# Two of eight tiles of a projection are moved ahead of the transposes that they stood behind

## The reference

```python
q, k, v = qkv_heads(h, w_qkv)                       # h @ w_qkv, 16 heads of 64
def one_chunk(c):                                   # 64 queries see a band of 9 chunks of keys
    s = jnp.einsum('bqhd,bkhd->bhqk', q_c, k_c).astype(jnp.float32) * scale + bias
    s = jnp.where(valid, s, NEG)
    p = jax.nn.softmax(s, axis=-1).astype(v.dtype)
    return jnp.einsum('bhqk,bkhd->bqhd', p, v_c)
```

## Time and profile before

| | |
|---|---|
| median of 3 runs | 2464.14 us (2463.99 to 2464.99) |
| profiled execution, its own time | 2464.97 us |
| its span, first to last instruction | 2463.2 us |
| granted clock of TensorE | 0.998 of full speed |
| busy: VectorE, ScalarE, POOL | 1546.7, 906.8, 231.2 us |

### The profile page before, as it was taken

One profiled execution on the slowest core, in us unless ns is written; L12 is line 12 of the kernel. 1 busy time (PEld: TensorE's weight loads), 2 busy tenths in 40 slices (PEclk: granted clock), 3 DMA queues, 4 the chain that ended last, 5 costly groups with the idle time before them and its releaser, 6 DMA issues.

```text
span 2463.2 us, 42975 instructions
## 1 busy us (share of the span) xinstructions
PE 2438.4 (99%) x16495; PEld 2392.2 (97%) x16495; DVE 1546.7 (63%) x2853; ACT 906.8 (37%) x1709; POOL 231.2 (9%) x535
## 2 busy tenths in 40 slices
PE   8999999999999999999999999999999999999998
PEld 8999999999999999999999999999999999999998
DVE  5666666677866666666666724427666666666666
ACT  6455545455433222222333641325222223322223
POOL 1011111103000000000000321221000000000000
PEclk9999999999999999999999999999999999999999
DMA  6122222444111111111111211112111111111112
GB/s 168 54 61 61 61 61 61 133 143 135 52 52 51 51 34 34 34 51 51 51 51 35 71 35 35 37 51 69 46 41 34 51 51 51 51 51 43 34 42 81
DMA packets 136522, 145.37 MB, mean 59 GB/s; under 512 B 4444, under 2 KB 125956, under 8 KB 136420
## 3 DMA queue, kind: packets, MB, share of 16 engines
q1 hardware_dynamic: 120420, 118.69, 15.2%
q0 software_dynamic: 14384, 23.03, 3.6%
q10 hardware_dynamic: 1616, 2.25, 0.3%
HBM read 125.97 MB, written 17.97 MB: 58 GB/s over the span
## 4 chain that ended last, share of the span: by engine, by line
PE 95%; DVE 2%; ACT 2%; issue 0%; DMA 0%; DVEq 0%; ACTq 0%
PE psum L170 29%; PE psum L169 29%; PE psum L171 29%; PE psum L1055 2%; PE psum L1075 2%; PE psum L1020 2%; PE psum L1984 1%; DVE w_lo L777 1%; DMA raw<-in_a_w_qkv 0%; PE psum L1968 0%; ACT w_hi L773 0%; PE psum L913 0%; ACT pB L1199 0%; ACT pA L1199 0%; DVE raw L2353 0%
## 5 line engine op out<-in xcount | busy, mean ns | idle before, releaser
L169 PE MATMUL psum<-gx_hi,w_hi 128*128 128x352 f32 x3456 | 1123.8, 325 | 1.3 <-DVE gx_lo L231 0.8
L170 PE MATMUL psum<-gx_lo,w_hi 128*128 128x352 f32 x3456 | 1116.3, 323 | 0.0
L171 PE MATMUL psum<-gx_hi,w_lo 128*128 128x352 f32 x3456 | 1115.2, 323 | 0.0
L169 PEld LDWEIGHTS psum<-gx_hi,w_hi 128*128 128x128 f32 x3456 | 649.8, 188 | 3.6 <-issue 1.0
L170 PEld LDWEIGHTS psum<-gx_lo,w_hi 128*128 128x128 f32 x3456 | 650.0, 188 | 0.6
L171 PEld LDWEIGHTS psum<-gx_hi,w_lo 128*128 128x128 f32 x3456 | 649.8, 188 | 0.0
L1743 DVE TENSOR_TENSOR x<-x,psum 128x352 f32<-128x352 f32 x528 | 258.4, 518 | 119.1 <-PE psum L171 118.9
L1614 ACT ACTIVATE conv_t<-a_gate,cur 128x352 f32<-128x352 f32 x132 | 89.9, 681 | 539.5 <-DVE a_gate L1694 532.3
L170 PE MATMUL psum<-h_loB,w_hi 128*128 128x352 f32 x528 | 171.1, 324 | 0.0
L171 PE MATMUL psum<-h_hiB,w_lo 128*128 128x352 f32 x528 | 171.0, 324 | 0.0
L170 PE MATMUL psum<-h_loA,w_hi 128*128 128x352 f32 x528 | 170.9, 324 | 0.0
(11 more groups left out here) (194 smaller groups left out, 2941.3 us busy)
## 6 DMA issues: line engine op xcount, KB each, us to landing
raw<-in_f_w_up SPq DMA_DIRECT2D x44, 1024.0 KB, 5.1
raw<-in_f_w_down SPq DMA_DIRECT2D x22, 1024.0 KB, 4.9
raw<-in_a_w_o SPq DMA_DIRECT2D x25, 512.0 KB, 4.0
raw<-in_a_w_qkv SPq DMA_DIRECT2D x22, 512.0 KB, 3.8
raw<-in_b_w_in SPq DMA_DIRECT2D x8, 1024.0 KB, 5.6
raw<-in_b_w_out SPq DMA_DIRECT2D x4, 1024.0 KB, 5.2
gx_hi<-o_scratch POOLq DMA_DIRECT2D x3, 1232.0 KB, 7.3
gx_lo<-o_scratch POOLq DMA_DIRECT2D x3, 1232.0 KB, 9.7
```

The costliest lines, as they stand in the source:

```text
L169: pe.matmul(out, w[0], rhs[0], start=first, stop=False)
L170: pe.matmul(out, w[0], rhs[1], start=False, stop=False)
L171: return pe.matmul(out, w[1], rhs[0], start=False, stop=last)
```

## The change

In steps that have no value products (step 1 and the even steps up to 62) the first two tiles of the projection are issued ahead of the first two groups of turns, the other six at the old place. `projection` takes the tiles as an argument; qkv_done is raised by the last tile. Both calls carry the waits for lin_out and at_lo. The work of the other engines is the same in the same order.

```diff
+    AHEAD = 2
+
...
-        def projection(t, s):
+        def projection(t, s, tiles):
 
             u, c = divmod(s, NCH)
             n = QKV0 + 3 * t + u
             pe.wait_ge(lin_out, STEPS * (t + 1) + s)
             pe.wait_ge(at_lo, n + 1)
-            linear(pe, psum[:, 7, :CH[c][1]], w_hi[n % 2], w_lo[n % 2], c).then_inc(qkv_done, 1)
+            mm = linear(pe, psum[:, 7, :CH[c][1]], w_hi[n % 2], w_lo[n % 2], c, None, tiles, KT - 1 in tiles)
+            if KT - 1 in tiles:
+                mm.then_inc(qkv_done, 1)
...
+            ahead = AHEAD if 1 <= g <= STEPS * LAST and not weighed(g) else 0
+            if ahead:
+                projection(*step_of(g - 1), range(ahead))
             if 1 <= g <= ALL:
                 turn(g - 1, range(min(2, len(key_groups((g - 1) % STEPS)))))
...
             elif g <= STEPS * LAST:
-                projection(*step_of(g - 1))
+                projection(*step_of(g - 1), range(ahead, KT))
```

## The result

The changed kernel took 2472.17 us (median of 8 runs, 2470.42 to 2472.97) against 2464.22 before (8 runs): 8.0 us more, a ratio of 1.0031 with a 95% interval of 1.0022 to 1.0040. Slower, by more than the forecast 6.7 us and inside the range. The profiled execution took 2472.04, 7.07 over that of before. Two of the twelve executions of experiment 2 took 6168 us, which no trace here explains, and are left out of its median.

What follows compares the result with a forecast made beforehand. TensorE, busy 99% of the span, was taken to bound the kernel. 3.4 + 1.3 + 1.7 + 0.3 = 6.7 us slower, on the median 2464.14 gives 2470.8; own range 2468.8 to 2472.8, with rivals 2467.0 to 2475.5.

Steps and rivals of the forecast that it cites:

- Eight waits 0.43 longer each: Steps 2, 8, 14, 26, 32, 44, 50, 62: TensorE waits for the eviction instead of the scaling, 3.4 us more.
- Seven steps that get a wait of their own: Steps 1, 10, 20, 28, 38, 46, 56: the eviction ends after the scores, so the projection starts late, 1.3 us together.
- The split: First TensorE instruction behind the scores loses 0.05 us more as a projection, in 32 steps: 1.7 us, bounds 0 to 3.5.
- Rival B: The split costs nothing in the touched steps: 5.0 us slower in all, 2469.1 us; chance 0.15.
- Step 1's late turns add 0.3 to step 2's wait: Step 1's exponentials come some 0.55 us late, TensorE 0.25: 0.3 us more waiting in step 2, between 0 and 0.5.
- The other late turns are hidden: ScalarE's 0.88 us wait for the maximum covers the 1.07 us delay but 0.2; odd steps, tightest 11, don't wait.
- rival C: The turns' delay runs on into odd steps 5, 11, 23, 29, 41, 47, 59: 4.7 us more, 2475.5; chance 0.09.
- Busy times stay, nothing is given back: Whole kernel: the engines' busy times stay the same and nothing later recovers the lost time.
- Rival A: Not slower: the two tiles fill the turns' wait, 4.1 us saved less 1.7 for the split, 2461.7; chance 0.06.

Runs made afterwards that it cites:

- experiment 2: The changed kernel with VectorE's scaling of a step put ahead of its split of weights: 2462.1 us.
- experiment 1: The kernel before, with VectorE's scaling put ahead of its split of weights in steps with s = 1, 4, 7: 2459.24 us, ratio 0.998.
- experiment 3: The changed kernel with the eviction of the projection ahead of the scaling on VectorE in steps with s = 1, 4, 7: 2463.41 us.
- experiment 4: The changed kernel, but two tiles go ahead only in the 17 even steps without any wait: 2465.09 us.
- experiment 7: The changed kernel with four tiles ahead of the turns instead of two: 2484.33 us.
- experiment 6: The kernel before with the change in step 62 alone: 2465.9 us.
- experiment 5: The changed kernel without the change in step 62: 2470.01 us.
- experiment 8: The kernel before, with POOL's first read-back of spilled results held until the scaling of step 61 is done: 2463.31 us.

## Why the prediction was right

- *Eight waits 0.43 longer each.* Right, to 0.03 us in seven of them (0.58 in step 2, see below), and by its cause: with the eviction's end moved ahead, by either of two edits on VectorE (experiments 1 to 3), the waits go.
- *Seven steps that get a wait of their own.* Right, 0.18 to 0.28 where 0.18 to 0.28 was forecast.
- *The split, 0.05 a step from the first instruction behind the scores.* Right: 0.045 by the 17 steps that have nothing else, in the changed kernel and in experiment 4. Rival B (no cost) falls by these 17 steps; over 32 steps the loss is 1.4, where the sum had 1.7. The Trainium skill ("TensorEngine Tiling (Array Packing)", section Key Properties) says only that changing the tiling mode drains TensorE and changing the tile doesn't; taken as the whole price, as in the prediction, it would give 0 here, and the runs don't bear that out.
- *Step 1's late turns add 0.3 to step 2's wait.* Too high: 0.60 - 0.48 = 0.12. Step 1's exponentials start 63.23 - 60.71 = 2.52 behind the first scores instead of 63.86 - 61.71 = 2.15, so 0.37 late and not 0.55. The turns were as late as forecast, but the copy started 0.42 behind them instead of 0.59, and the exponentials into its end.
- *The other late turns are hidden.* Right: step 4's exponentials came 0.02 late and step 11's turns did not wait. The margin in step 11 is thin, if wider than I said: 0.22 us are left from the scaling's end to the turn, of which a wait would take 0.05. With the scaling behind the eviction it is gone (experiment 3), with four tiles too (experiment 7). There my account of what waits behind the exponentials was incomplete, and the price of rival C with it.
- *Busy times stay, nothing is given back.* Right for the other engines; TensorE is busy for 2.0 us more. A price for the clock was missing: the sum put it at nothing, without saying so. Without it the attention grew by 8.0 - 1.6 = 6.4, which is what the forecast of 6.7 stands against; the lowest runs differ by 2470.42 - 2463.99 = 6.4 too. The medians differ by 8.0: the profiled execution lost 1.6 to the clock behind step 62's wait, and the other runs' times, most of them near 2472, suggest the same of them. That 2472.17 still lies in the range is luck, for its bounds were made of the split and of step 2. Of the three profiled executions with the longer wait, two show half clock in step 62 (the changed kernel and experiment 7), one doesn't (experiment 6); of the seven others none does. So the fall goes with that wait; why it comes in one execution and not in another stays open.

Rival A was the change's intent; experiment 3 shows that the eviction's place was what kept the tiles from covering the waits. Even so it came out 0.8 under the kernel before, which its interval doesn't tell from nothing, where A would have given 2.4: A left out the odd steps' 1.1 us and some 0.6 in steps 1, 10, 28 and 46, where the eviction still ends late.

## What to carry to other kernels

Before filling one engine's wait with other work, look up in the releaser's own queue when the filler's permission comes: a filler whose wait is released by a later instruction of the same queue makes the wait longer. Ask next why the releaser is late; here it stood behind 1.2 us of work that nobody needed yet, and putting it ahead won 5 us where filling lost 8. And a longer wait of a nearly always busy engine can cost more than itself: here a wait of 1.84 or 1.85 us was followed by half clock in two of three profiled executions, at 1.6 us more.

## What the runs showed of the hardware

- The granted clock fell to 1.2 GHz in step 62 of the changed kernel after a wait of 1.85 us (0.50 in the stretch from 484.20 to 487.50) and was back in the next (1.00 from 487.60 to 489.00). In the stretch at half clock, turns went from 0.11 to 0.21 apart and projection matmuls from 0.16 to 0.29, 1.6 us in all. With a wait of 1.42 (before, experiments 4 and 5) it did not fall there in the profiled executions; with 1.84 it did in the one of experiment 7 and didn't in the one of experiment 6.
- A scaling on VectorE takes 0.90 and 1.05 us instead of 0.55 while POOL issues two DMAs (1.00 and 0.98). The Trainium skill ("SBUF — State Buffer", section "Who interferes with whom") says that such an instruction (tensor_scalar) can enter a mode in which it and GpSimd contend for a shared pair of ports, and that the one that issues second is then blocked in full. No run shows which mode the scaling was in. Experiment 8 agrees that the two disturb each other, but not in full: the first scaling starts 0.60 us before POOL's first issuing ends and loses 0.35, the second 0.76 before the second one's end and loses 0.50.
